# One core, fp32r: small projection columns as 24 stationary columns of rounded weights and remainders, and decode output rows as 40 stationary columns

## The reference, cut to what matters

```
h = rms_norm(x, norm_w)                       # (tokens, 1024)
proj = h @ w_in + b_in                        # 9740 columns, split among the branches
beta = sigmoid(dn_b); log_alpha = -exp(dn_A_log) * softplus(dn_a + dn_dt_bias)
logf = log_sigmoid(ff)                        # dn_b, dn_a, ff: 4 columns each
...
merged = sum(gates * up, axis=2)              # (tokens, 1024)
y = x + merged @ w_out                        # (tokens, 1024)
```

## Time and profile before

| | before |
|---|---|
| median of 3 runs | 1666.29 us (1665.57 to 1668.97) |
| the profiled execution | 1669.67 us, its span 1668.0 us |
| PE busy / DVE / ACT / POOL, share of the span | 97% / 53% / 32% / 30% |
| mean granted TensorE clock | 0.995 of full speed |

### The profile page before, as it was taken

The page is one execution under the profiler, slowest core; times in us unless marked ns, Lnnn a source line. Parts: engine busy times, 40 slices in busy tenths (PEclk is TensorE's granted clock), DMA queues, the critical chain, the costliest instruction groups (busy, mean ns, idle before and its releaser), DMA issues. The chain is left out here.

```text
span 1668.0 us, 26092 instructions
## 1 busy us (share of the span) xinstructions
PE 1612.3 (97%) x10579; PEld 1541.0 (92%) x10579; DVE 884.0 (53%) x1288; ACT 537.4 (32%) x934; POOL 502.6 (30%) x379
## 2 busy tenths in 40 slices
PE   5999999999999999999999999999999999999999
PEld 4989989999999999998889899999999999889976
DVE  4667853344444442790387672435657552995611
ACT  6323243222222222233334443321145223664200
POOL 2333415333343411911244551222212121103400
PEclk9999999999999999999999999999999999999999
DMA  4211155223222114542366352235210341535521
GB/s 156 53 26 41 44 155 135 71 71 70 71 70 71 51 49 121 149 127 63 99 191 188 104 177 107 65 115 158 71 39 14 108 109 55 164 118 152 152 77 58
DMA packets 189365, 163.16 MB, mean 98 GB/s; under 512 B 18381, under 2 KB 157056, under 8 KB 188727
## 3 DMA queue, kind: packets, MB, share of 16 engines
q1 hardware_dynamic: 189246, 161.51, 33.4%
HBM read 131.38 MB, written 30.22 MB: 97 GB/s over the span
## 5 line engine op out<-in xcount | busy, mean ns | idle before, releaser
L276 POOL TENSOR_TENSOR wL<-w_raw,wH 128x1024 fp32r<-128x1024 f32 (+1 forms) x112 | 238.4, 2129 | 803.1 <-ACT wH L269 803.0
L335 PE MATMUL ps<-hH,wH 128*128 128x344 f32 x1920 | 458.2, 341 | 12.6 <-PEq L196 3.6
L335 PE MATMUL ps<-hL,wH 128*128 128x344 f32 x1920 | 420.1, 321 | 0.0
L335 PE MATMUL ps<-hH,wL 128*128 128x344 f32 x1920 | 419.4, 321 | 0.0
L335 PEld LDWEIGHTS ps<-hH,wH 128*128 128x128 f32 x1920 | 316.7, 190 | 26.5 <-issue 10.7
L335 PEld LDWEIGHTS ps<-hL,wH 128*128 128x128 f32 x1920 | 327.3, 189 | 0.2
L335 PEld LDWEIGHTS ps<-hH,wL 128*128 128x128 f32 x1920 | 324.9, 189 | 0.0
L269 ACT ACTIVATE wH<-w_raw 128x1024 fp32r<-128x1024 f32 (+1 forms) x116 | 108.5, 936 | 117.6 <-PE ps L335 107.2
L2918 POOL TENSOR_SCALAR fa_logits<-fox_c_bc,token_scalars 128x128 f32<-128x128 f32 (+7 forms) x32 | 58.7, 1834 | 51.9 <-DMA fox_c_bc<-rows_g_c_beta 27.0
L1880 ACT ACTIVATE d_m<-ps 128x512 f32<-128x512 f32 x48 | 28.7, 598 | 134.8 <-PE ps L2062 134.8
L1268 DVE SCALAR_TENSOR_TENSOR m_th<-m_th,ps 128x1032 f32<-128x1032 f32 x24 | 29.5, 1228 | 61.9 <-PE ps L335 61.9
(11 more groups left out here) (576 smaller groups left out, 2783.9 us busy)
## 6 DMA issues: line engine op xcount, KB each, us to landing
w_raw<-in_w_in SPq DMA_DIRECT2D x80, 512.0 KB, 5.1
m_th<-gate_spill SPq DMA_DIRECT2D x28, 516.0 KB, 4.5
gate_spill<-d_gate SPq DMA_DIRECT2D x18, 516.0 KB, 3.0
fa_kv<-in_cache_fox_k SPq DMA_DIRECT2D x32, 256.0 KB, 3.1
fa_kv<-in_cache_fox_v SPq DMA_DIRECT2D x32, 256.0 KB, 3.4
w_raw<-in_w_branch SPq DMA_DIRECT2D x32, 256.0 KB, 2.9
gate_spill<-fa_gate SPq DMA_DIRECT2D x10, 516.0 KB
x_rows<-in_x_prompt SPq DMA_DIRECT2D x8, 512.0 KB, 6.3
```

What stands on the lines that cost most here:

```text
L276: pool.tensor_tensor(self.wL[:, t % 2, 0:nk], self.raw_at(t)[:, 0:nk], self.wH[:, t % 2, 0:nk].bitcast(F32), ALU.subtract).then_inc(self.w ...
L335: last = pe.matmul(self.ps[:, b + g, 0:cols], w[:, t % 2, k], x[:, k, g * cols:(g + 1) * cols], start=(k == 0 and n == 0), stop=(k == nk - ...
```

## The change

`SmallColumns`: rounded weights and remainders lie side by side in `WHL`, 24 columns for each block `k`, and are one stationary operand. The passes are two (`hH`, `hL`) instead of three; 24 PSUM rows come out, of which the upper 12 are the remainders' part. The result of ACT (`Z`) has 24 rows, the transposes give 24 columns for a token tile, and DVE adds the two halves with `tensor_reduce` where it copied before. POOL fills the factor column by three `affine_select` instead of one short memset. The product of remainder and remainder is now in the sum.

`merge_and_output`: the decode tokens' rounded values (columns 0 to 7) and their remainders (columns 32 to 39) lie in `ROWS`, 40 columns for each `k`, zero between them. A decode unit is 8 x 2 matmuls; DVE adds PSUM rows 32 to 39 in an operation of its own before the add of all units.

```diff
@@ -597,9 +597,10 @@
...
-        self.W, self.WH, self.WL = sb("sw", [P, KD, M]), sb("swH", [P, KD, M], F32R), sb("swL", [P, KD, M], F32R)
-        self.col = sb("sw_cols", [M, 8])
-        self.Z = K.merged[0:M, KD - 1]
+        self.W, self.WHL = sb("sw", [P, KD, M]), sb("swHL", [P, KD, 2 * M], F32R)
+        self.WH, self.WL = self.WHL[:, :, 0:M], self.WHL[:, :, M:2 * M]
+        self.col = sb("sw_cols", [2 * M, 8])
+        self.Z = K.merged[0:2 * M, KD - 1]
...
@@ -609,9 +610,9 @@
...
-        self.turned = K.ps[:, self.BANK, 0:(TT8 + 1) * M].rearrange("p (t c) -> p t c", c=M)
-        self.sums = K.ps[:, self.BANK, 128:128 + TT8 * 2 * H].rearrange("p (t c) -> p t c", c=2 * H)
-        self.rows = K.ps[0:TT8 * 3 * H, self.BANK, 256:256 + P]
+        self.turned = K.ps[:, self.BANK, 0:(TT8 + 1) * 2 * M].rearrange("p (t c) -> p t c", c=2 * M)
+        self.sums = K.ps[:, self.BANK, 256:256 + TT8 * 2 * H].rearrange("p (t c) -> p t c", c=2 * H)
+        self.rows = K.ps[0:TT8 * 3 * H, self.BANK, 384:384 + P]
...
@@ -625,8 +626,10 @@
...
-        pool.wait_ge(prep, 2)
-        pool.memset(col[0:4, 3:4], 1.0).then_inc(prep, 1)
+        for n, (upto, fill) in enumerate(((self.M + 4, 1.0), (self.M, -1.0), (4, 1.0))):
+            pool.wait_ge(prep, 2 + n)
+            pool.affine_select(out=col[:, 3:4], in_=col[:, 3:4], compare_op=ALU.is_ge, fill=fill, base=-upto,
+                               pattern=[[0, 1]], channel_multiplier=1).then_inc(prep, 1)
 
     def sync_loads(self, sp):
         i, col, loaded = self.K.i, self.col, self.N["loaded"]
@@ -662,14 +665,14 @@
...
+        act.activation(self.WH, self.W[:], ACT.Identity).then_inc(N["split"], 1)
         act.activation(self.FAC[:], self.FAC[:], ACT.Exp).then_inc(N["split"], 1)
...
-        act.activation(self.Z.rearrange("p (a b) -> p a b", a=3), self.K.ps[0:self.M, 3:6, 0:G3], ACT.Identity,
+        act.activation(self.Z.rearrange("p (a b) -> p a b", a=3), self.K.ps[0:2 * self.M, 3:6, 0:G3], ACT.Identity,
                        scale=col[:, 3:4], bias=col[:, 4:5]).then_inc(N["z"], 1)
 
     def act_values(self, act):
@@ -691,9 +694,9 @@
...
-        dve.wait_ge(N["prep"], 3)
+        dve.wait_ge(N["prep"], 5)
         dve.wait_ge(N["split"], 2)
-        dve.tensor_tensor(self.WL[:], self.W[:], self.WH[:].bitcast(F32), ALU.subtract).then_inc(N["split"], 1)
+        dve.tensor_tensor(self.WL, self.W[:], self.WH.bitcast(F32), ALU.subtract).then_inc(N["split"], 1)
         dve.scalar_tensor_tensor(col[:, 4:5], col[:, 0:1], col[:, 3:4], col[:, 1:2], ALU.mult, ALU.add
...
@@ -704,8 +707,10 @@
...
-        v.step(dve.tensor_copy(T[:, 0:TT8], self.turned[:, 0:TT8]))
-        v.do(dve.tensor_copy(T[0:NB, TT8], self.turned[0:NB, TT8]))
+        v.step(dve.tensor_reduce(T[:, 0:TT8], self.turned[:, 0:TT8].rearrange("p t (x c) -> p t c x", x=2),
+                                 AX.X, ALU.add))
+        v.do(dve.tensor_reduce(T[0:NB, TT8], self.turned[0:NB, TT8].rearrange("p (x c) -> p c x", x=2),
+                               AX.X, ALU.add))
         v.do(dve.tensor_scalar(flat(T1), flat(T), -1.0, None, ALU.mult))
         dve.tensor_tensor(flat(T1), flat(T1), flat(T), ALU.min).then_inc(N["t1"], 1)
...
@@ -721,18 +726,18 @@
...
-            for n, (w, x) in enumerate(((self.WH, K.hH), (self.WH, K.hL), (self.WL, K.hH))):
+            for n, x in enumerate((K.hH, K.hL)):
                 for g in range(3):
-                    last = pe.matmul(K.ps[0:self.M, 3 + g, 0:G3], w[:, k], x[:, k, g * G3:(g + 1) * G3],
-                                     start=(k == 0 and n == 0), stop=(k == KD - 1 and n == 2))
+                    last = pe.matmul(K.ps[0:2 * self.M, 3 + g, 0:G3], self.WHL[:, k], x[:, k, g * G3:(g + 1) * G3],
+                                     start=(k == 0 and n == 0), stop=(k == KD - 1 and n == 1))
         last.then_inc(N["done"], 1)
...
         for t in range(TT8):
-            pe.transpose(self.turned[:, t], self.Z[:, t * P:(t + 1) * P], K.ident[0:M, 0:M])
-        pe.transpose(self.turned[0:NB, TT8], self.Z[:, SEQ:TOK], K.ident[0:M, 0:M]).then_inc(N["tr"], 1)
+            pe.transpose(self.turned[:, t], self.Z[:, t * P:(t + 1) * P], K.ident[0:2 * M, 0:2 * M])
+        pe.transpose(self.turned[0:NB, TT8], self.Z[:, SEQ:TOK], K.ident[0:2 * M, 0:2 * M]).then_inc(N["tr"], 1)
 
     def pe_sums(self, pe):
 
@@ -1355,9 +1360,11 @@
...
+        ROWS = sb("o_decode_rows", [P, KD, 32 + NB], F32R)
         X = m.TH[:].rearrange("p s t -> p (s t)")[:, 0:NX * HALF].rearrange("p (s c) -> p s c", s=NX)
...
+        rows, clear = K.sem("o_rows"), K.sem("o_rows_clear")
         block = K.block
...
@@ -1404,6 +1411,8 @@
                 for e in range(4):
                     m.pool(pool, m.branch[2 * e] + 2)
                     weights(e)
+                    if e == 0:
+                        pool.memset(ROWS[:].bitcast(F32), 0.0).then_inc(clear, 1)
...
@@ -1427,6 +1436,8 @@
...
+                act.wait_ge(clear, 1)
+                act.activation(ROWS[:, :, 0:NB], K.merged[:, :, SEQ:TOK], ACT.Identity, scale=0.5).then_inc(rows, 1)
                 for e in range(4, KD):
                     weights(e)
...
@@ -1440,17 +1451,32 @@
...
+                dve.wait_ge(rows, 1)
+                dve.scalar_tensor_tensor(ROWS[:, :, 32:32 + NB], K.merged[:, :, SEQ:TOK], 0.5,
+                                         ROWS[:, :, 0:NB].bitcast(F32), ALU.mult, ALU.subtract).then_inc(rows, 1)
+                v = K.V(dve)
                 for u, (_, t) in enumerate(units):
                     n = rows_of(t)
+                    x = X[0:n, u % NX]
                     dve.wait_ge(x_in[u % NX], 16 * (u // NX + 1))
                     dve.wait_ge(done, u + 1)
-                    dve.tensor_tensor(X[0:n, u % NX], K.ps[0:n, bank(u)], X[0:n, u % NX], ALU.add).then_inc(y, 1)
+                    if t == TT8:
+                        v.do(dve.tensor_tensor(x, K.ps[32:32 + NB, bank(u)], x, ALU.add))
+                    dve.tensor_tensor(x, K.ps[0:n, bank(u)], x, ALU.add).then_inc(y, 1)
 
             @block.tensor
             def _(pe):
                 def part(u, ks, begin, end):
                     e, t = units[u]
                     n = rows_of(t)
+                    if t == TT8:
+                        pe.wait_ge(rows, 2)
+                        for k in ks:
+                            for w in (WH, WL):
+                                last = pe.matmul(K.ps[0:32 + NB, bank(u)], ROWS[:, k], w[e][:, k],
+                                                 start=(k == 0 and w is WH), stop=(k == KD - 1 and w is WL))
+                        last.then_inc(done, 1)
+                        return
                     passes = [(k, x, w) for k in ks for x, w in ((K.hH, WH), (K.hL, WH), (K.hH, WL))]
...
```

More of the change, by code:

```diff
@@ L664, in act_split @@
         act.wait_ge(N["loaded"], 16 * 8)
-        act.activation(self.WH[:], self.W[:], ACT.Identity).then_inc(N["split"], 1)
+        act.activation(self.WH, self.W[:], ACT.Identity).then_inc(N["split"], 1)
         act.activation(self.FAC[:], self.FAC[:], ACT.Exp).then_inc(N["split"], 1)
```

## The result

The changed kernel took 1660.26 us (median of 6 runs, 1659.3 to 1661.79), the kernel before 1666.39 us in the same sessions (6 runs, 1665.57 to 1670.81): -6.1 us, ratio 0.9962 with a 95% interval of 0.9949 to 0.9975. The forecast was 1659.7 us, -6.64.

A forecast was written before the change was run, and what follows sets the result against it. PE, busy 97% of the span, bounds the kernel, through a chain from tile 4's end and the final output matmuls. -3.76 + 0.11 - 3.71 + 0.72 = -6.64 us takes the median from 1666.29 to 1659.65; range 1657.3 to 1663.3.

The forecast's parts named there:

- Pace of the small matmuls, -3.76: Small matmuls inside tile 4 on PE: 24 of 72 go, at 0.157 us each, so -3.76 us.
- the reduces, +0.11: Small values on DVE: reduces replace copies, +0.10 and +0.01 for the small one; bounds 0 and +0.43 us.
- Width costs nothing: Stationary block of small matmuls grows from 12 to 24 columns; pace stays 0.157 us, the load lying behind the running matmul.
- The turns and the selects hidden: Tile 5's wider transposes (0 to +0.7 us) and POOL's three selects (+0.2 to +0.9) covered by idle times: 0.
- Output, -3.71 and +0.72: Last merge: 16 decode matmuls fewer at 0.232 us, -3.71 us; a second dependent add at the end, +0.72 us.
- Nothing in it is held by something that the change leaves at its old time: Chain from tile 4's end to 152.02 us through PE, ACT, DVE and SP: if tile 4 ends earlier, all of it moves.
- the wait for the transfer unchanged in length: ACT's 5.04 us wait for weights behind SP's small stores keeps its length, ending near 148.4 us for 152.02.
- rival 1: PE's clock halves after some idle times, 1.7 us each; one drop more gives 1661.4, one fewer 1658.0; chance 0.12, evenly.
- Rival 4: Eleven idle times of PE get clock drops, 1.7 us each; six drops give +3.6 us, 1669.9; chance 0.04.

The follow-up runs named there:

- the two kernels with the load first: Tile 9's weights loaded ahead of the small stores on SP, in the kernel before (1665.56 us, ratio 0.9990) and in the changed kernel (1660.02 us, ratio 0.9957).
- the output part alone: Changed kernel with the small columns put back to three passes as before, keeping the new decode units: 1665.08 us, ratio 0.9988 to before.
- the kernel before with the load first: Kernel before with one thing moved, tile 9's weights loaded ahead of the small stores on SP: 1665.56 us, ratio 0.9990 to before.
- three passes: Changed kernel with three passes of the 24-column block in place of two, 72 small matmuls as before: 1664.26 us, ratio 0.9977 to before.
- small part only: Kernel before with only the changed kernel's class `SmallColumns`, output as before: 1663.47 us, ratio 0.9979 to before.
- wide: Changed kernel with stationary blocks padded by zero columns, 128 for small matmuls and 104 for decode units: 1658.36 us, ratio 0.9948 to before.
- decode unit early: Changed kernel with the second half's decode unit done second in its half instead of last: 1659.6 us, ratio 0.9948 to before.
- all three edits: Changed kernel with tile 9's load ahead of the stores, sums one block later in tile 6, second half's decode unit second: 1659.0 us, ratio 0.9957.

## Why the prediction was right

- **Pace of the small matmuls, -3.76, and the reduces, +0.11:** 0.156 us each, 103 ns and 13 ns more; the two kernels with the load first differ by 3.67 us in the stage.
- **Width costs nothing:** shown with 128 and 104 columns.
- **The turns and the selects hidden:** the wider turns made ACT's move of tile 5 come 0.11 us later after tile 4's (116.11 - 99.56 = 16.55 us for 120.11 - 103.67 = 16.44). At tile 6 (127.07 for 131.08) only the reduces' 0.11 is left of the side work (the move is 3.68 us earlier in the stage, for 3.79 at tile 4), since PE waits at the sums anyway. The selects made the first convolution start 53.14 - 50.86 = 2.28 us after `sw_cols`'s memset for 52.65 - 51.19 = 1.46 before, +0.8, near the upper bound; DVE's idle time before the third convolution took it, 1.37 us for 2.24.
- **Output, -3.71 and +0.72:** the end measured -2.94 to -2.98 for -2.99.
- **A step that failed:** "Nothing in it is held by something that the change leaves at its old time", and with it "the wait for the transfer unchanged in length". ACT's wait for tile 9's weights went from 5.04 to 2.41 us, and PE's 2.65 us behind it to none. The link through SP is not a fixed length that moves with the chain. From the first small store to the next load of weights it was 12.32 us before, 11.74 with the output part alone and 12.62 in the kernel before with the load first, where the issue of the eight stores ended last; it was 9.35 to 9.93 in the nine others, three passes among them, where the landing of the four row stores did. In the profiles, the changed kernel's stage lost 4.2 us beyond its own 3.67 (7.87 in all). Over three more profiles of kernels with the short stores (small part only, wide, decode unit early) the part beyond is 3.2 to 3.6.
- **The median does not show that extra**, -6.1 for -6.64; with 4.2 us more it would be -10.8, outside the interval (-4.2 to -8.5). The two profiles of before and changed differ by 8.9 us, more than the medians. In these two the clock took part of it back, rival 1 (the rest is 2.3 us longer in the changed kernel's profile). The table's rest, which no edit touches, runs from 1312.9 us with 3.4 us at half clock to 1321.8 with 20.6: 8.9 us for 17.2, about half of it. The number of such stretches changed from profile to profile. PE's stretches with a drop, in the changed kernel:

```profile
264.00:272.00 8.00, 6.25 (x35) 0.79 0.36 100
760.00:768.00 8.00, 6.44 (x33) 0.79 0.58 152
1408.00:1416.00 8.00, 7.58 (x40) 0.79 0.60 193
```

With all three edits there is only one between 200 and 1500 us, at 1400 to 1408. The first of the changed kernel's stood behind an idle time of 1.75 us, at 267.66. An idle time of that length had no drop in the trace of before; at 753.56 us there even one of 1.85 had none. The other way round, the idle time of 2.08 us at 840.80 us had a drop in the profile of before, and the same one at 833.18 us in the changed kernel's had none. So the mechanism of rival 1 is there, in both directions, a few us either way in one execution. Over all twelve profiles a drop followed 17 of the 23 idle times of PE from 1.95 to 2.1 us, 7 of the 25 from 1.7 to 1.8, and 7 of the 102 from 1.3 to 1.7. The Trainium skill ("TensorE: Matmul & The Clock Gate", Part 1) says that where the clock changes differs between runs of one kernel; these traces, one for each kernel, can't show that for one kernel, but agree with it in that like idle times were followed by a drop in one and not in another. Whether the shift of this change makes drops more frequent on the whole, these runs don't show: 2 in the rest of before, 3 in the changed kernel's, 1 to 6 in the others'.
- **What the clock does to the runs:** the mean granted clock of nearly every run is on record. Of 17 runs of the kernel before in one session the fastest, 1662.0 us, had 0.999 and the slowest, 1674.77 us, 0.989. Lines of one slope through the runs of each kernel (162 runs with a granted clock over 0.98) give 1.1 us for 0.001 of clock. An estimate, from the times brought to one clock by that slope and compared with before on the same chip: small part -3.8 us, output part -3.0, wide blocks (the whole change) -7.3, three passes -2.6, and -0.8 for the kernel before with the load first, each with a standard error of 0.4 to 0.5. So both parts are worth what the sum said. The stall at tile 9, 4.46 us in the one profile of before, is beside the clock some 1 us of its average execution, and the output's gain, which the plain ratio leaves open, is clear of the noise.
- **Luck:** that -6.1 lies so near to -6.64 is in part luck. The shorter wait, which the sum didn't have, adds some 1 us to the gain, and the changed kernel's six runs had a mean granted clock of 0.995, for 0.996 in the 67 later runs of before, which by that slope takes 1.1 us off it. (The clocks of the six runs of before that stand beside them are not on record.)
- Rival 4 (slower by drops) did not come about.

## What to carry to other kernels

When a stationary operand fills few columns, put rounded part and remainder side by side: a pass over the moving operand is saved, and the added columns are free as long as the load lies behind the matmul. Price such an edit by the start-to-start pace at its own place, and look for what is next on its chain: a small store queued ahead of a weight load carries any delay of its own, and the wait for its landing where something reads it back, to the bounding engine. Where a change is worth less than 0.5%, compare lengths of stages in the profiles beside the medians, count the time at half clock, and set each run's time beside its mean granted clock before explaining what is left.

## What was not expected of the hardware

- A DMA issue of a 2 KB store took 4.6 us on SP while the trace shows no DMA traffic (131 to 134 us), with eight such issues taking 7.4 to 10.4 us in four profiles and 3.7 us in eight.
- The time at half clock in the same stretch of program ranged from 3.4 to 20.6 us over twelve profiles.
